# Two blocks on one core: form steps two at a time, the last heads' turns three steps behind attention

## What is computed

```python
h = rmsnorm(x, norm1_g[l])
p = jnp.einsum('bsd,de->bse', h, w_in[l])
u = p[..., :c0]                                   # pooling mixer
dq, dk, dv = jnp.split(p[..., c0:c1], 3, axis=-1)  # differential attention
sq, sk, sv = jnp.split(p[..., c1:], 3, axis=-1)    # stick-breaking attention
a_out = pool_mixer(u, pool_w[l], pool_scale[l])
b_out = diff_attention(...)
c_out = stick_breaking_attention(...)
mix = jnp.concatenate([a_out, b_out, c_out], axis=-1)
x = x + jnp.einsum('bse,ed->bsd', mix, w_out[l])
h2 = rmsnorm(x, norm2_g[l])
x = x + jnp.einsum('bsf,fd->bsd', jax.nn.silu(h2 @ w_gate) * (h2 @ w_up), w_down[l])
```

## Time and profile before

| | us |
|---|---|
| median of 3 runs | 3676.12 (3675.49 to 3677.59) |
| the profiled execution's own time | 3679.37 |
| its span, first to last instruction | 3677.6 |
| PE, PEld, DVE, ACT, POOL busy | 3512.9, 2934.5, 2129.1, 1148.8, 1754.2 |

### The profile page before, as it was taken

The page is one execution under the profiler, slowest core; times in us unless marked ns, Lnnn a source line. Parts: engine busy times, 40 slices in busy tenths (PEclk is TensorE's granted clock), DMA queues, the critical chain, the costliest instruction groups (busy, mean ns, idle before and its releaser), DMA issues.

```text
span 3677.6 us, 51937 instructions
## 1 busy us (share of the span) xinstructions
PE 3512.9 (96%) x22042; PEld 2934.5 (80%) x22042; DVE 2129.1 (58%) x2739; ACT 1148.8 (31%) x1913; POOL 1754.2 (48%) x1260
## 2 busy tenths in 40 slices
PE   8999999988999999999999999999999899999998
PEld 7788888867778787877878888777788778787876
DVE  7845566377364545456774466657778255545454
ACT  2122212266222222223122122336666222222223
POOL 4332334549255555556333324632588245545454
PEclk9999999999999999999999999999999999999999
DMA  3111313554101111113111132361231201101111
GB/s 124 36 36 36 143 52 102 176 144 140 58 23 54 50 53 51 54 50 144 46 35 36 35 149 81 121 211 58 64 108 57 72 23 37 67 35 69 36 68 64
DMA packets 79690, 275.82 MB, mean 75 GB/s; under 512 B 9057, under 2 KB 9313, under 8 KB 76900
## 3 DMA queue, kind: packets, MB, share of 16 engines
q1 hardware_dynamic: 70816, 242.25, 19.7%
q10 hardware_dynamic: 8642, 30.24, 2.1%
HBM read 224.23 MB, written 48.23 MB: 74 GB/s over the span
## 4 chain that ended last, share of the span: by engine, by line
PE 76%; DVE 14%; ACT 4%; POOL 3%; issue 2%; DMA 0%; SPq 0%; POOLq 0%; DVEq 0%; ACTq 0%
PE ps L1429 21%; PE ps L1430 20%; PE ps L1431 20%; PE ps L1435 4%; PE ps L1730 2%; PE ps L1700 2%; PE ps L1701 2%; PE ps L1735 2%; DVE acc L2127 1%; DVE af_hi_p L2126 1%; DVE tf_lo_p L2126 1%; ACT wd_hi L1784 1%; DVE af_lo_p L2126 1%; PE ps L1505 1%; DVE rhf L2126 1%
## 5 line engine op out<-in xcount | busy, mean ns | idle before, releaser
L2721 POOL TENSOR_TENSOR ring_lo<-ring_raw,ring_hi 128x512 fp32r<-128x512 f32 (+1 forms) x362 | 613.6, 1700 | 377.3 <-ACT ring_hi L1784 367.2
L1429 PE MATMUL ps<-a_hi,ring_hi 128*128 128x512 f32 x1472 | 590.7, 401 | 29.5 <-DVE af_hi_p L2126 16.5
L1430 PE MATMUL ps<-a_lo,ring_hi 128*128 128x512 f32 x1472 | 577.3, 392 | 0.0
L1431 PE MATMUL ps<-a_hi,ring_lo 128*128 128x512 f32 x1472 | 576.9, 392 | 0.0
L1429 PEld LDWEIGHTS ps<-a_hi,ring_hi 128*128 128x128 f32 x1472 | 278.5, 189 | 103.9 <-DVE af_hi_p L2126 24.1
L1431 PEld LDWEIGHTS ps<-a_hi,ring_lo 128*128 128x128 f32 x1472 | 278.5, 189 | 60.5
L1430 PEld LDWEIGHTS ps<-a_lo,ring_hi 128*128 128x128 f32 x1472 | 278.9, 189 | 54.3
L2126 DVE TENSOR_TENSOR xres<-xres,ps 128x512 f32<-128x512 f32 x352 | 234.8, 684 | 149.4 <-PE ps L1431 147.4
L1429 PE MATMUL ps<-wd_hi,af_hi 128*128 128x512 f32 x704 | 277.8, 395 | 23.4 <-DVE xres L2126 17.5
L2722 POOL TENSOR_SCALAR ring_hi<-ring_raw 128x1024 fp32r<-128x1024 f32 x84 | 108.5, 1291 | 360.3 <-PE ps L1431 311.3
L1430 PE MATMUL ps<-wd_lo,af_hi 128*128 128x512 f32 x704 | 276.6, 393 | 0.0
(11 more groups left out here) (305 smaller groups left out, 8055.9 us busy)
## 6 DMA issues: line engine op xcount, KB each, us to landing
ring_raw<-w SPq DMA_DIRECT2D x92, 512.0 KB, 3.5
ring_raw<-wgu SPq DMA_DIRECT2D x68, 512.0 KB, 3.6
uq<-q_scr SPq DMA_DIRECT2D x96, 256.0 KB, 4.8
ring_raw<-wd SPq DMA_DIRECT2D x34, 512.0 KB, 3.6
ring_raw<-wo SPq DMA_DIRECT2D x32, 512.0 KB, 3.6
uk<-k_scr SPq DMA_DIRECT2D x6, 2048.0 KB, 10.4
rlf<-wgu SPq DMA_DIRECT2D x20, 512.0 KB, 4.5
xraw<-xt SPq DMA_DIRECT2D x16, 512.0 KB, 7.4
```

The lines of the kernel that those rows point to most:

```text
L1429: pe.matmul(o, ah, bh, start=begin and i == 0, stop=False)
L1430: pe.matmul(o, ah, bl, start=False, stop=False)
L1431: last = pe.matmul(o, al, bh, start=False, stop=end and i == len(pairs) - 1)
L2721: tt = lambda o, a, b, op: pool.tensor_tensor(o, a, b, op=op)
```

## The change

Two numbers in the plan. The input's forms of the second block get two steps a round instead of one, and the flips left in `tail` are emitted three steps after attention's end instead of eight. No operation is added, removed or resized; positions in the queues change, in both halves.

```diff
@@ -1026,7 +1026,7 @@
             env["pool"] = True
 
         forms = plan_forms(hf, 0, lambda: ("turned", 1) in env, lambda: "pool" in env, env["marks", 0])
-        return [(dense2(), 1), (pool(), 1), (forms, 1)]
+        return [(dense2(), 1), (pool(), 1), (forms, 2)]
 
 
     def plan_attention(hf, env):
@@ -1282,7 +1282,7 @@
                 if len(tail) > 1:
                     tail.pop(0)[1]()
             env["attn"] = True
-            for _ in range(8):
+            for _ in range(3):
                 yield True
                 while settle:
                     _, k, v = settle.pop(0)
```

## The result

The changed kernel takes **3645.41 us** (median of 4 runs, 3643.0 to 3647.2) against 3675.8 (4 runs, 3671.37 to 3677.59) for the kernel before on the same chip: ratio 0.9917, 95% interval 0.9905 to 0.9929. That is 30.4 us faster (26 to 35 by the interval).

What follows compares the result with a forecast made beforehand. TensorE, busy 96% of the span, was taken as the bound, so only its waits could yield time. Gains 5.2 + 4.0 + 3.0 + 3.1 + 3.1 + 3.1 + 1.7 = 23.2, less 1, gave 22 and 3654 us; range 3647 to 3667.

Steps and rivals of the forecast that it cites:

- the clock's term of the sum: Lower TensorE clock in the 8 us behind the four waits: 3.0, 3.1, 0 and 1.7 us, expected to come back.
- The four waits: PE waits at the second block's first-pair third product, 5.98 and 5.31 us, and before projection tile 4, 3.11 us per half.
- The factor of 1.9 beside POOL: In `xform1`, DVE operations running beside POOL were taken to need 1.9 times as long as alone.
- the rival on the slower side: ACT's form copies hold the sq0 and sk0 evacuations, so PE stalls at sv0's tiles: up to 3678 us, chance 0.03.
- The splits near 966: POOL's gu0000, gu0001 and gu0010 splits, released by the flip, would run about 966 to 976.4 instead of from 973.78, free.
- the late form of sk1: sk1's first two forms, behind sv0's late spill and two weight loads, would start near 581, wanted at 601: no cost.
- (b): Rest of z = 1's forms at 562 to 576, partly beside POOL's dv0 split: 3.2 us more for POOL, 3.3 us cover.
- the rule of the Trainium skill: Two-input DVE operations and GpSimd reads exclude each other for a whole instruction: second pooling sum 4 us late, not about 1.
- the residue of the long waits: What stays of the waits at the first pair's third product: about 0.7 us in half 0, 1.2 in half 1.
- the step "I take off 1": 1 us off the 23.2 us sum, because remainders and short waits elsewhere may meet the clock differently.
- part 2: Moving the last head's flip ahead of turn 1: 3.1 us of waiting gained in each half, 1.7 of clock in half 1.
- The cover of 24 matmuls: Between the flip's transposes and tile 4, 24 matmuls (5.4 us) and a turn would cover the 3.11 us wait.

Runs made afterwards that it cites:

- e1_forms: The kernel before with only the first edit, the input's forms two steps a round, the last head's flip left where it was: 3655.94 us, ratio 0.9951.
- e2_flip: The kernel before with only the second edit, the flip emitted three steps after attention's end, the forms left at one a step: 3666.09 us, ratio 0.9973.
- e8_shift: The changed kernel with 12 matmuls of no use ahead of the first pair's third product in each half: 3652.62 us, ratio 0.9939.
- e5: The changed kernel with the flip one place later, behind tile 3's second half but still ahead of turn 1: 3645.6 us, ratio 0.9924.
- e7: The changed kernel with four more DVE subtractions ahead of t1's form in each half: 3666.14 us, ratio 0.9978.
- e12: As e9, but one and two form operations by turns in the rounds of the plain products: 3638.82 us, ratio 0.9902 to the kernel before.
- e9: The changed kernel with the second block's feed-forward forms one a round until the plain products end, then two: 3645.45 us, ratio 0.9923.
- e4: The kernel before with 22 matmuls of no use ahead of the first pair's third product in both halves: 3668.16 us, ratio 0.9981.

## Why the prediction was wrong in size

The failed step is the clock's term of the sum: 3.0 + 3.1 + 0 + 1.7, less 1, is 6.8 us, and 13.5 us came back beyond the waiting. The waiting itself was put at 15.4 us and was 16.9. The mechanism held.

**What held.** The four waits, their releasers and what ends them. With the shift of 1.67 us taken off, `xform1` was forecast at 595.0 and started at 594.87; the subtraction was forecast at 610.2 and started at 609.93. The factor of 1.9 beside POOL held: the last four operations, worth 4.4 us alone, took 8.4. The low parts of sq0 and sk0 ended at 548.91 and 554.81, within 0.2 us of the forecast 550.4 and 556.4 once the shift is taken off, so the rival on the slower side had nothing to stand on; the pooling sum started 0.1 us late, not 1. The splits near 966 (on the old time scale) and the late form of sk1 came as forecast, at no cost. No rival took place.

On (b), the rule of the Trainium skill (SBUF — State Buffer, Who interferes with whom) can be seen in the rows: four DVE operations worth 4.9 us took 9.5 beside POOL's splits, 4.6 more, close to the 4 us that I had worked out by it. Each of the four ended 1.1 us behind the end of a POOL operation (POOL's ended at 565.31, 568.63, 570.62 and 573.95, DVE's at 566.37, 569.71, 571.69 and 575.03), as if it had waited for that one and then run alone. But they ran in an idle stretch of 11.61 us, and the sum behind them did not come late, so the rule's price was paid out of the idle time. POOL's two splits took 3.4 us longer than before (10.5 against 7.0). I had put 3.2, where the rates that I named (0.8 more for a low part, a high one doubled) add up to 3.8.

**What failed.** First, the residue of the long waits: I left 0.8 and 1.3 us and found 0.29 and 0.31, so 10.7 us are gone and not 9.2. Most of these 1.5 us lie in half 1, where I let 5.1 us of DVE's work run beside POOL, from 2313.33 on. The rows show the same last four operations there as in half 0: the first slow one starts at 2294.72, 8.4 us ahead of the subtraction at 2303.12, and they are worth 4.4 us alone. POOL's splits had not moved against PE (2293.82 against 2312.84, 19.0 us earlier, like PE's pooling matmuls, 2284.70 against 2303.72), and both halves end alike.

Second, and larger, the step "I take off 1". The clock behind the four places was 3.0 + 3.1 + 0 + 1.7 = 7.8 in my sum; the second profile of before gives 2.7 + 1.4 + 0 + 1.7 = 5.8, so 7.8 was not too little. But 30.4 less 16.9 of waiting leaves 13.5 us. Some 6 to 8 us therefore came back at waits that the change does not touch, where I had expected them to go the other way, if anything (by the interval of the result it is at least 1 us over 16.9 + 7.8). The clocks of all runs bear out the size (16 us less loss, some of it inside the removed waits), and both parts show such a surplus: e1_forms gained 19.9 against 10.7 of waiting and 6.1 to 6.8 of clock, e2_flip 9.8 against 6.2 and 1.7. Of the whole, 3.4 us stand at the two 2.66 us waits: all four profiles with the old order of the forms lost 1.6 us or more at each, the three of the changed kernel nothing, and e8_shift, which lost there again, took 2.5 us more than its added work. Where the rest came from, and why the loss at those two went, is not settled; two profiles of one kernel differ by more.

The range failed by the same step: its low end allowed for two other short waits without their 1.7 us, and it would have taken three or four.

The waiting that part 2 removes was right (6.2 us). The cover of 24 matmuls that I gave as the reason is enough, but most of it was not needed: e5 shows that the flip's place ahead of turn 1, in ACT's queue and PE's, was worth 2.4 of each 3.11 us.

## What to carry to other kernels

Where PE is busy for 96% of the span, price a removed wait at its own length plus the clock behind it, and then look at all kernels' runs for the clock and not at one profile: here each us of waiting came with 1.6 to 1.9 us of time where the whole wait went or came back (e1, e2, e7). Helper work belongs where its engine is idle and nothing waits behind it; the same pace that was right in one stage held up the next, so find the operation that PE waits for and count what stands ahead of it in its queue. Shortening a long wait gives the clock back only if what is left is short enough: cut from 6.88 to 4.73 us (e12) the wait kept its loss, cut to 2.30 (e9) it had none, nor had what was left of 1.01 and less (e4, where the rest was filled, and e5). That is no threshold: the waits of 2.66 us lost clock in some profiles and not in others.

## What was not expected of the hardware

- The clock's loss behind one and the same wait differs between runs of one kernel: 3.1 and 1.4 us behind 5.31 us, 1.7 or nothing behind 3.11 and 2.66 us. The Trainium skill (TensorE: Matmul & The Clock Gate, Part 1) says of the start of a kernel that the number of slow matmuls varies from run to run; the traces show it behind waits in the middle as well. The same page puts the penalty of that start under 1% of a typical span. Here the first 150 us show no loss at all (clock 1.00 in both kernels' first profiles), and the losses of the whole run are 1.5% before (0.9852) and 1.1% after. Some 4 us of them lie in the last ten us or so, in which PE has no work; the rest stands behind waits in between.
- 22 matmuls of no use in a wait made a kernel 7.7 us faster.
- Waits of 0.3 to 1.0 us at these places were followed by a clock of 1.00 in every window taken.
- Each of four two-input DVE operations beside POOL's splits ended 1.1 us behind the end of a POOL operation (above, on (b)).
